# The delta rule of a two-layer hybrid block: subtract the old values first, then solve

## The reference, cut to what matters

```
kb = k * beta[..., None]
m = where(strict, einsum('bhnid,bhnjd->bhnij', kb, k) * decay, 0)
a = m + eye(L)
rhs = concatenate([v * beta[..., None], kb * exp(G)[..., None]], -1)
sol = triangular_solve(a, rhs, lower=True, unit_diagonal=True)
w_val, k_cd = sol[..., :dv], sol[..., dv:]
attn = einsum('bhnid,bhnjd->bhnij', q, k) * decay
def step(st, inp):
    qd, kcd, wv, at, kt, gt = inp
    v_new = wv - einsum('bhld,bhde->bhle', kcd, st)
    o = einsum('bhld,bhde->bhle', qd, st) + einsum('bhij,bhje->bhie', at, v_new)
    st = st * gt[..., None, None] + einsum('bhld,bhle->bhde', kt, v_new)
    return st, o
```

## Time and profile before

| | us |
|---|---|
| median of 3 runs | 3154.51 (3153.37 to 3157.71) |
| the profiled execution | 3156.76 |
| its span, first to last instruction | 3154.0 |
| the delta block in it | about 1822 to 2196 |
| a stage of it, k = 1 to 7, by the starts of line 2470 | 37.8 to 40.5 |

### The profile page before, as it was taken

One profiled execution on the slowest core, in us unless ns is written; L12 is line 12 of the kernel. 1 busy time (PEld: TensorE's weight loads), 2 busy tenths in 40 slices (PEclk: granted clock), 3 DMA queues, 4 the chain that ended last, 5 costly groups with the idle time before them and its releaser, 6 DMA issues. The chain is left out here.

```text
span 3154.0 us, 53100 instructions
## 1 busy us (share of the span) xinstructions
PE 3022.1 (96%) x22610; PEld 2893.4 (92%) x22610; DVE 1601.1 (51%) x2734; ACT 733.6 (23%) x1425; POOL 1087.2 (34%) x731
## 2 busy tenths in 40 slices
PE   8999999999999999999999969996999999999995
PEld 7999668999999999999999958885999999999995
DVE  2338674744444344487665546552563444334456
ACT  2213473310110101123222145552121011010113
POOL 2233101252223332327523147774453223223230
PEclk9999999999999999999999979997999999999998
DMA  6220102011111111113332144322311111111101
GB/s 172 51 56 7 47 1 85 14 54 47 41 41 41 54 54 41 42 34 119 97 97 85 57 117 102 82 69 61 95 38 47 47 41 44 45 41 47 41 28 58
DMA packets 264865, 184.44 MB, mean 58 GB/s; under 512 B 49801, under 2 KB 249847, under 8 KB 264631
## 3 DMA queue, kind: packets, MB, share of 16 engines
q1 hardware_dynamic: 264631, 181.06, 19.8%
HBM read 147.19 MB, written 33.84 MB: 57 GB/s over the span
## 5 line engine op out<-in xcount | busy, mean ns | idle before, releaser
L148 PE MATMUL ps<-xhi,whi 128*128 128x364 f32 (+1 forms) x3504 | 1160.9, 331 | 18.8 <-POOL wlo L1403 15.0
L149 PE MATMUL ps<-xlo,whi 128*128 128x364 f32 (+1 forms) x3504 | 1155.9, 330 | 0.0
L154 PE MATMUL ps<-xhi,wlo 128*128 128x364 f32 (+1 forms) x3504 | 1155.0, 330 | 0.0
L148 PEld LDWEIGHTS ps<-xhi,whi 128*128 128x128 f32 (+1 forms) x3504 | 660.0, 188 | 24.1 <-POOL wlo L1403 16.6
L149 PEld LDWEIGHTS ps<-xlo,whi 128*128 128x128 f32 (+1 forms) x3504 | 660.2, 188 | 3.2 <-issue 0.3
L154 PEld LDWEIGHTS ps<-xhi,wlo 128*128 128x128 f32 (+1 forms) x3504 | 659.4, 188 | 1.4
L1400 POOL TENSOR_SCALAR whi<-wraw 128x1024 fp32r<-128x1024 f32 x168 | 189.2, 1126 | 1236.7 <-PE ps L154 1236.3
L1956 DVE TENSOR_TENSOR z<-ps,z 128x364 f32<-128x364 f32 x432 | 232.0, 537 | 575.4 <-PE ps L154 575.4
L1403 POOL TENSOR_TENSOR wlo<-wraw,whi 128x1024 fp32r<-128x1024 f32 x168 | 431.1, 2566 | 14.0
L148 PE MATMUL ps<-eo_hhi,whi 128*128 128x364 f32 x528 | 174.7, 331 | 0.0
L148 PE MATMUL ps<-oo_hhi,whi 128*128 128x364 f32 x528 | 174.7, 331 | 0.0
(11 more groups left out here) (400 smaller groups left out, 4445.5 us busy)
## 6 DMA issues: line engine op xcount, KB each, us to landing
wraw<-in_w_ff_in SPq DMA_DIRECT2D x88, 512.0 KB, 3.9
wraw<-in_w_ff_out SPq DMA_DIRECT2D x44, 512.0 KB, 3.4
qkvz<-eo_ob SPq DMA_DIRECT2D x32, 546.0 KB, 4.7
wraw<-in_w_in_o SPq DMA_DIRECT2D x32, 512.0 KB, 4.6
z<-residual SPq DMA_DIRECT2D x6, 1456.0 KB, 7.9
wraw<-in_w_in_e SPq DMA_DIRECT2D x17, 512.0 KB, 4.0
residual<-z SPq DMA_DIRECT2D x3, 1456.0 KB, 6.7
dn_gb<-gates SPq DMA_DIRECT2D x34, 128.0 KB, 3.7
```

Of the source, the lines that this page charges most:

```text
L148: one = pe.matmul(out, whi, xhi, start=start, stop=False)
L149: two = pe.matmul(out, whi, xlo, start=False, stop=False)
L154: return pe.matmul(out, wlo, xhi, start=False, stop=stop)
```

## The change

Since T(beta v) - T(beta e^G k) S = T beta (v - (e^G k) S), the keys need not be solved: the state is multiplied with decayed keys, that is subtracted from the plain values, and the difference is solved once. The factor beta of the rows moves onto T's columns (in the masks `low` and `ups`, whose factors change places) and onto the product's rows in `new_values`. The parts:

- PE: lines 2545 and 2550 at the stage's end go. `solve(B, b)` comes after each `old_values(B, b)`: TT times the difference, 8 matmuls of 64x128 for each chunk. The turn of the values stands before `ksum` now, and `ksum` waits until T of the pair before is complete.
- DVE: `residue(B, b)` (values minus product) is new before each `new_values(B, b)`, which now waits for the solve and multiplies by beta.
- ACT: the 8 scalings into `kbg` (line 2623), the two copies into `kc` (line 2661) and the copy `Tv` (line 2666) go; the 8 scalings into `vb` (line 2603) become one copy into `vt`. The preparation of `bcol` goes.
- POOL: `scaled_keys(A)`, two products of keys and e^G, is new between `decayed(B, 0)` and `levels_of(A, (1,))`.
- `kc`, the values and TT get two buffers each. SP waits for `low_b` where it waited for `ups_b`, and for `kc` before it loads the keys of C.

```
 # POOL
+            def scaled_keys(A):
+                pool.wait_ge(s("kn"), A.th(1, 1))
+                pool.wait_ge(s("eg"), A.th(1, 1))
+                if A.k >= 2:
+                    pool.wait_ge(s("kS"), A.th(-2, 2))
+                for b, r in enumerate(A.blocks()):
+                    ins = pool.tensor_tensor(kc[A.odd][:, :, r]..., kk[:, b]..., eg[:, b]..., ALU.mult)
+                ins.then_inc(s("kc"), 1)
 # PE
             def old_values(B, b):
                 pe.wait_ge(s("kc"), B.th(1, 1))
-                pe.wait_ge(s("Tv"), B.th(1, 1))
+                if not B.first:
+                    pe.wait_ge(s("oln"), B.th(0, 1))
+            def solve(B, b):
+                pe.wait_ge(s("r"), B.th(b + 1, 2))
+                pe.wait_ge(s("TT"), B.th(B.group(LEVELS - 1, b), 2 * LEVELS))
+                for h, half, j in places(b):
+                    ins = pe.matmul(bank2(0)[half, j, :], TT[B.odd][half, j, :], vt[B.odd][half, j, :], ...)
+                ins.then_inc(s("Tr"), 1)
             def run(A, B, C):
                 if A:
+                    pe.wait_ge(s("in2"), A.loaded())
+                    turn(A, 4, kv, "vturned")
                     pe.wait_ge(s("sqk"), A.th(1, 1))
+                    if not A.first:
+                        pe.wait_ge(s("TT"), A.th(0, 2 * LEVELS))
                     ... ksum ...
-                    turn(A, 4, kv, "vturned")
                 if B:
                     old_values(B, 0)
+                    solve(B, 0)
...
                 if B and B.n == P:
                     old_values(B, 1)
+                    solve(B, 1)
...
-                            pe.wait_ge(s("kbg"), A.th(1, 1))
...
-                    for b in range(A.nb): ... kbg with TT ... "kcd"
-                    for b in range(A.nb): ... TT with vb ... "TvP"
 # ACT
-                    for j in range(A.J): act.mul(vb[:, j, :], bank2(4)[:, j, :], beta) ... "vb"
+                    if A.k >= 2:
+                        act.wait_ge(s("Tr"), A.th(-2, 2))
+                    act.copy(vt[A.odd][:, 0:A.J, :], bank2(4)[:, 0:A.J, :]).then_inc(s("vt"), 1)
-                    ... act.mul(kbg[:, j, :], bank2(6)[:, j, :], bcol) ... "kbg"
-                    act.wait_ge(s("kcd"), A.th(1, 1)) ... act.copy(kc...) ... "kc"
-                    act.wait_ge(s("TvP"), A.th(1, 1)) ... act.copy(kbg...) ... "Tv"
 # DVE
             def new_values(B, b):
+                dve.wait_ge(s("Tr"), B.th(b + 1, 2))
+                dve.tensor_tensor(vn[:, hs, :], bank2(0)[:, hs, :], beta.to_broadcast([P, GR, P]), ALU.mult)
+            def residue(B, b):
+                dve.wait_ge(s("vt"), B.th(1, 1))
                 dve.wait_ge(s("kS"), B.th(b + 1, 2))
-                dve.tensor_tensor(vn[:, hs, :], kbg[:, hs, :], bank2(0)[:, hs, :], ALU.subtract)
+                dve.tensor_tensor(v, v, bank2(0)[:, hs, :], ALU.subtract).then_inc(s("r"), 1)
```

More of the change, by code:

```diff
@@ L2196, in delta_block @@
         AT = (AT0, AT1)
-        kbg, vb, kc, vn, Sg = (sb(n, [P, H, P]) for n in ("kbg", "vb", "kc", "vn", "Sg"))
+        vt = (sb("vt0", [P, H, P]), sb("vt1", [P, H, P]))
+        kc = (sb("kc0", [P, H, P]), sb("kc1", [P, H, P]))
+        vn, Sg = (sb(n, [P, H, P]) for n in ("vn", "Sg"))
         ktl = (sb("ktl0", [P, H, P]), sb("ktl1", [P, H, P]))
@@ L2358, in run @@
                 if A:
+                    scaled_keys(A)
                     levels_of(A, (1,))
@@ L2407, in old_values @@
                 for h, half, j in places(b):
-                    ins = pe.matmul(bank2(0)[half, j, :], kc[:, h, r], S[b][:, h, :], start=True, stop=True)
+                    ins = pe.matmul(bank2(0)[half, j, :], kc[B.odd][:, h, r], S[b][:, h, :], start=True, stop=True)
                 ins.then_inc(s("kS"), 1)
@@ L2415, in old_values @@
                     pe.matmul(bank2(2)[:, h, r], S[b][:, h, :], kq[B.odd][:, h, r], start=h % GR == 0, stop=False)
+            def solve(B, b):
+                pe.wait_ge(s("r"), B.th(b + 1, 2))
+                pe.wait_ge(s("TT"), B.th(B.group(LEVELS - 1, b), 2 * LEVELS))
+                for h, half, j in places(b):
+                    ins = pe.matmul(bank2(0)[half, j, :], TT[B.odd][half, j, :], vt[B.odd][half, j, :], start=True, stop=True)
+                ins.then_inc(s("Tr"), 1)
             def state_step(B, b, A):
                 if A:
-                    pe.wait_ge(s("vb"), A.th(1, 1))
+                    pe.wait_ge(s("vt"), A.th(1, 1))
                 pe.wait_ge(s("vn"), B.th(b + 1, 2))
@@ L2527, in run @@
                                 for h, half, j in places(b):
[L2528 removed]
+                                    pe.matmul(bank1(6 + b)[half, j - GR * b, :], TT[A.odd][half, j, :], X[half, j, :],
                                               start=True, stop=True)
                             for h, half, j in places(b):
[L2531 removed]
+                                ins = pe.matmul(bank1(6 + b)[half, GR + j - GR * b, :], X[half, j, :], TT[A.odd][half, j, :],
                                                 start=True, stop=True)
@@ L2535, in run @@
                             squares_sum(B)
[L2537 to L2551, removed]
                 elif B:
@@ L2611, in run @@
                     act.copy(egl[:, A.odd, 0:nb, :], eg[:, 0:nb, :, L - 1:L].squeeze(3)).then_inc(s("egl"), 1)
[L2613 to L2623, removed]
-                                          m.bcol[:, bass.ds(A.index, 1), j:j + 1].squeeze(1))
-                    ins.then_inc(s("kbg"), 1)
                 if B and not A:
@@ L2657, in run @@
                     act.activation(m.xhi[:, :, bass.ds(B.col, B.n)], rt[:, :, 0:B.n], ACT.Copy).then_inc(s("ohi"), 1)
-                if A:
-                    act.wait_ge(s("kcd"), A.th(1, 1))
-                    for g in range(2):
-                        ins = act.copy(kc[:, HALVES[g], 0:n].rearrange("p h (b c) -> p h b c", c=L),
-                                       bank1(4 + g)[:, 0:A.J, :].rearrange("p (b h) c -> p h b c", h=GR))
-                    ins.then_inc(s("kc"), 1)
-                    act.wait_ge(s("TvP"), A.th(1, 1))
-                    act.copy(kbg[:, 0:A.J, :], bank2(0)[:, 0:A.J, :]).then_inc(s("Tv"), 1)
-            act.activation(m.bcol[:, :, :], m.gcol[:, :, 0:HEADS], ACT.Exp).then_inc(s("egcol"), 1)
             squares_k(Pair(0))
@@ L2710, in run @@
                 if B:
+                    residue(B, 0)
                     new_values(B, 0)
@@ L2730, in run @@
                 if B and B.n == P:
+                    residue(B, 1)
+                if A:
+                    dve.tensor_tensor(tt[:, 0:J], tt[:, 0:J], masked(m.EYE, J), ALU.add).then_inc(s("TT0"), 1)
+                if B and B.n == P:
                     new_values(B, 1)
                 if A:
-                    dve.tensor_tensor(TT[:, 0:J], TT[:, 0:J], masked(m.EYE, J), ALU.add).then_inc(s("TT0"), 1)
                     dve.wait_ge(s("kturned"), A.th(1, 1))
```

43 lines of the change are left out of this document (20 added, 23 removed).

## The result

The changed kernel took 3183.27 us (median of 4 runs, 3182.64 to 3183.68). Beside it, before took 3156.11. The ratio is 1.0089 with a 95% interval of 1.0076 to 1.0102: slower by 0.9%. The prediction was 3186, slower.

What follows compares the result with a forecast made beforehand. POOL's chain through `xlo` to the next key norm was taken as the bound; the lengthened loop, start and end gave +17.8 us, the low clock +14.0, together +31.8, so 3186.3 us, range 3165 to 3197.

Steps and rivals of the forecast that it cites:

- What bounds the kernel: Loop between stages: POOL's chain through `xlo` to the next key norm takes 38.02 us, tied with PE's own list.
- the middle: Between key scale and squaring: the subtraction and two solves add 2.5 us per stage, making the loop 40.5 us.
- The end of a stage: PE's removed lines 2545 and 2550, 3.82 us per full stage, were worth nothing on the deciding chain.
- The last pair: Last of the seven turns: 1.4 us goes off because norm and key scale are half as large, leaving 282.1 us.
- PE's new gap and the clock: Before the first solve: PE idle 5.1 us, clock falls to 0.50, costing 2.0 us in each of stages 2 to 8, +14.0.
- The start: Start of the block: `ksum` about 5.3 us later behind the values' turn, offset by removed work; -1.5, between -4 and +2.
- The ends: Two solves in stage 8, +2.2 us; in the last stage a solve at low clock and `new_values`, +2.7 us.
- `scaled_keys` and the shared port: POOL's new products fit in idle time and new DVE operations wait for none: 0; by the port rule up to 9 us.

Runs made afterwards that it cites:

- fill: Changed kernel with PE kept busy before the first solve: chunk 0's decayed-key products made four times, two unread rounds added; 3177.74 us, ratio 1.0066.
- rfirst: Changed kernel with the subtraction of chunk 0 put ahead of the key scale in DVE's queue; 3168.42 us, ratio 1.0034.
- before_own: Kernel before the change, with the key norm in a buffer of its own so it does not wait for POOL's `xlo`; 3155.91 us, ratio 0.9997.
- own_late: Changed kernel with the key norm in its own buffer and ACT's rounding of the output moved behind the next key norm; 3158.79 us, ratio 1.0007.
- own_rfirst: own_late and rfirst together, on the changed kernel; 3152.02 us, ratio 0.9986.
- best: own_rfirst with `ksum` put ahead of the turn of the values for the first pair; 3146.85 us, ratio 0.9973.
- own: Changed kernel with the key norm in a buffer of its own, so it does not wait for POOL's `xlo`; 3169.79 us, ratio 1.0038.

## Why the prediction was right, step by step

**What bounds the kernel, and the middle.** Right. The loop at full clock was put at 40.5 us; the first turn of after took 40.44, two of `fill` 40.48 and 40.47. POOL's `xlo` ended 22.25 to 22.29 after the squaring began in the full stages, 22.35 to 22.53 in before. The norm was released by `xlo` seven times. The subtraction and first solve (1.55) and the second solve (1.05) are measured one by one in `rfirst`. One thing the prediction did not see, since it read the norm of stage 7 alone: before the change, `xlo` released the norm in stages 2 and 7 only. In 0, 1 and 3 to 6 PE's sum did, 0.5 to 2.3 us behind the end of `xlo` in stages 3 to 6. The waits of ACT's key norm in before's block:

```profile
ACT dn_rt L2596 <- PE ps L2470: 7.3, 6, 2.8
```

Stage 7 was thus one of two in which PE had not fallen behind. Reading it as the loop's bound was right for after, where PE has 3.82 us less to do at the stage's end, and it is why `before_own` gained nothing.

**The end of a stage, worth 0.** Right: PE's removed 3.82 us became part of the wait in front of the solve. It was not gone for good; `own_late` and `own_rfirst`, in which PE decides, are what collects it.

**The last pair.** This term was mis-sized. "1.4 goes off because the last pair is half as large" counted the norm and the key scale only. POOL's six masks are half-sized too (0.73 instead of 1.26 for most), and they stand in the 22.36 us: from squaring to `xlo` the last turn took 19.47, so it was 2.8 us shorter again. Seven turns at full clock are thus 279.2 and not 282.1. The chain was read in stage 6 and then taken to be the same in all stages. In before stage 8's norm did not wait for this chain, so the waits did not show the saving; the timeline did, with 19.28 from squaring to `xlo` in stage 7. These are two of the masks, on POOL, in that turn of after:

```profile
2150.51 0.73 POOL L2331 TENSOR_TENSOR dn_low<-dn_low,masks 128x256 f32<-128x256 f32 x1
2151.20 0.73 POOL L2333 TENSOR_TENSOR dn_ups<-dn_upi,masks 128x256 f32<-128x256 f32 x1
```

**PE's new gap and the clock.** The mechanism is right and `fill` shows it. The gap was 3.8 to 4.6 us in five of the stages 2 to 8, 2.49 in stage 5 and 1.52 in stage 8, not 5.1: PE's stalls at issue and its own slower work in the same stage ate the rest. Its cost was 1.4 to 2.0 us in each of the stages 2 to 7, 1.7 on average, where I took 2.0. Of seven turns' +21.8 us, 10.3 are this, and the loop itself gives the other 11.5.

**The start** was put at -1.5; the key scale of stage 1 ended 1.34 earlier. In this trace the first squares were also ready 1.15 later than in before's (1831.30 against 1830.15), so counted from them the start gained 2.5. Its two parts were there: the first norm 6.4 us later, less work at the end of stage 0. That the new order of turn and sum costs 5 us by itself was priced at 5.3, and `best`, which takes it back, is 5.2 faster than `own_rfirst`.

**The ends.** Stage 8 was put at 2.2, and 2.0 for its share of the clock; from its key scale to level 1 it is 13.27 now against 9.83, so +3.4. The last stage was put at +2.7. From the squaring of stage 8 to that of the last stage, on ACT, after and then before:

```profile
2178.02 1.03 ACT L2583 ACTIVATE dn_sq<-ps 128x1024 f32<-128x1024 f32 x1
2212.18 0.60 ACT L2583 ACTIVATE dn_sq<-ps 128x512 f32<-128x512 f32 x1 [19.46 <-PE ps L2457]
```
```profile
2154.11 1.03 ACT L2571 ACTIVATE dn_sq<-ps 128x1024 f32<-128x1024 f32 x1
2185.75 0.60 ACT L2571 ACTIVATE dn_sq<-ps 128x512 f32<-128x512 f32 x1 [13.40 <-PE ps L2430]
```

34.16 against 31.64: +2.5. The measured terms are -1.3 + 21.8 + 3.4 + 2.5 = 26.4 of the 27.9. The remaining 1.5 comes behind that last squaring. There the clock is back up 24.0 us after it (at 2236.2), and was back after 22.0 before; that this accounts for it was not tested.

So the forecast of +31.8 stood 3.9 above the 27.9 by these misses: 2.9 of the turns at full clock (nearly all of it the last pair), 1.7 of the clock in stages 2 to 7, 0.8 in stage 8 and 0.2 in the last stage were too much, 0.2 at the start and the 1.5 behind the block, which no term priced, too little. The closeness of 3186 to the measured 3183.27 has a little luck in it: misses of either sign met, and before ran 1.6 us higher beside after (3156.11) than in the runs on which the forecast stood (3154.51); the difference of the medians is 27.2.

**`scaled_keys` and the shared port, worth 0.** Right. POOL's product starts 0.73 after the key scale and is done 3.2 after it, and the 15 subtractions and the 14 products of the new form took 683 and 692 ns on average in the seven turns:

```profile
L2687 DVE TENSOR_TENSOR dn_vt<-dn_vt,ps 128x512 f32<-128x512 f32 x15 | 10.2, 683 | 1.3 <-PE ps L2427 1.3
L2678 DVE TENSOR_TENSOR dn_vn<-ps,gcol 128x512 f32<-128x512 f32 x14 | 9.7, 692 | 17.6 <-PE ps L2441 17.6
```

I had put the rule too widely. The Trainium skill, page SBUF — State Buffer, section "SBUF: two separate sides", gives it for a VectorE operation in a mode that uses two ports, or with two inputs in SBUF, and the latter only against a GpSimd operation that reads SBUF. Both new operations have an input in PSUM, and agree with it.

## What to carry to other kernels

When work is taken from one of two tied chains, ask whether the other holds it, and measure the tie by taking the link away in both versions: here a second buffer is worth 13 to 16 us after the change and nothing before it. A change that loses can be worth keeping once the new idle time is put to use; the operation that a new first step waits for should be looked at in its queue, as a subtraction standing behind one it does not need cost 1.5 us a stage. A stretch in which TensorE waits costs twice when its clock falls with it, so price the wait and the slower work separately.

## What was not expected of the hardware

**Short gaps can cost the clock, and need not.** In after a gap of 1.52 us (stage 8) and one of 2.49 (stage 5) were followed by a clock of 0.50, as those of 4.6 were. A gap of 1.20 left it up in six stages of `own_late`, but not in a seventh, and left it up in stage 1 of after and of `own`; it was lost behind such a gap in stage 1 of `fill` and stage 7 of `own`. One of 3.10 left it up in stage 4 of `rfirst`. The length of the gap alone did not tell.

**A key scale beside POOL.** In `own` the key scale, whose inputs are both in SBUF, runs beside POOL's scaling of the state, and both get longer on average; in the full stages of after they do not overlap. The groups of the seven turns, of `own` and then of after (busy us, mean ns of one):

```profile
L2357 POOL TENSOR_TENSOR dn_Sg<-dn_S,dn_egl 128x1024 f32<-128x1024 f32 x14 | 30.5, 2179 | 4.6 <-DVE dn_S L2690 4.6
...
L2703 DVE TENSOR_TENSOR dn_k<-dn_k,dn_kr 128x1024 f32<-128x1024 f32 x6 | 9.5, 1588 | 29.4 <-ACT dn_kr L2609 29.4
```
```profile
L2357 POOL TENSOR_TENSOR dn_Sg<-dn_S,dn_egl 128x1024 f32<-128x1024 f32 x14 | 26.5, 1895 | 4.6 <-DVE dn_S L2692 4.6
...
L2705 DVE TENSOR_TENSOR dn_k<-dn_k,dn_rt 128x1024 f32<-128x1024 f32 x7 | 8.6, 1226 | 49.2 <-ACT dn_rt L2611 49.2
```

1588 against 1226 ns, and 2179 against 1895. The one that starts later is the one that gets longer: in stage 3 of `own` POOL's scaling starts 0.45 us ahead and takes its usual 1.90, and the key scale takes 2.53; in stage 7 the key scale starts 0.06 ahead and takes 1.22, and POOL's scaling 2.91. In after they overlap once, in stage 8: the half-sized key scale took 0.92 us there, and 0.69 in before.
